# One FP32 inference step on one core: the input projection by seven half-size products in place of eight, and two cache copies issued at another place

## The reference

```
h = rmsnorm(x, norm_mix)                  # (576, 1024): 512 prompt rows, 64 sample rows
z = h @ w_in                              # w_in: (1024, 3072)
q1, q2, k1, k2, va, qb, kb, vb = split(z) # rope on q1, q2, k1, k2, qb, kb
# differential attention on q1..va, dilated window attention on qb, kb, vb
x = x + even_merge(oa, ob) @ w_out        # output projection, (1024, 1024)
x = x + hier_moe(rmsnorm(x))              # top-1 of 4 groups, top-2 of 8 experts; then layer 1
```

## Time and profile before

| | |
|---|---|
| three runs | median 1953.74 us (1950.34 to 1958.75) |
| the profiled execution | 1954.98 us, its span 1953.0 us |
| TensorE products, busy | 1652.9 us (85%) |
| VectorE, ScalarE, GpSimd, busy | 647.7, 329.2, 215.5 us |
| DMA | 659.20 MB, mean 338 GB/s |
| granted TensorE clock, mean | 0.928 |

### The profile page before, as it was taken

The page is one execution under the profiler, slowest core; times in us unless marked ns, Lnnn a source line. Parts: engine busy times, 40 slices in busy tenths (PEclk is TensorE's granted clock), DMA queues, the critical chain, the costliest instruction groups (busy, mean ns, idle before and its releaser), DMA issues.

```text
span 1953.0 us, 32634 instructions
## 1 busy us (share of the span) xinstructions
PE 1652.9 (85%) x12820; PEld 784.3 (40%) x12820; DVE 647.7 (33%) x1326; ACT 329.2 (17%) x753; POOL 215.5 (11%) x356
## 2 busy tenths in 40 slices
PE   8999898888898887887788879998968887877785
PEld 4444355555445322222223347764532222323231
DVE  3213468777514300000000159984160000000005
ACT  2000245444302000000000020004120000000001
POOL 1001122232200100000000021000020000000000
PEclk9999989899898899999989889999979999999997
DMA  9999489999853899999999999704169999999995
GB/s 341 346 362 349 176 307 336 348 355 366 345 220 135 321 428 428 410 429 427 427 427 428 415 267 324 248 13 170 65 251 426 428 419 422 427 428 428 427 422 210
DMA packets 83830, 659.20 MB, mean 338 GB/s; under 512 B 15308, under 2 KB 15437, under 8 KB 45419
## 3 DMA queue, kind: packets, MB, share of 16 engines
q1 hardware_dynamic: 58906, 569.86, 73.5%
q0 software_dynamic: 24800, 87.65, 11.8%
HBM read 643.18 MB, written 96.53 MB: 379 GB/s over the span
## 4 chain that ended last, share of the span: by engine, by line
PE 55%; DMA 32%; DVE 7%; issue 3%; ACT 2%; SPq 1%; DVEq 0%; ACTq 0%; POOLq 0%
DMA ring<-in 31%; PE ps L2113 15%; PE ps L1758 10%; PE ps L2068 7%; PE ps L2276 6%; PE ps L1716 4%; PE ps L1882 2%; PE ps L2297 2%; PE ps L2133 2%; PE ps L1867 1%; DVE ring L1238 1%; PE ps L1822 1%; DVE ring L1231 1%; PE ps L1798 1%; DMA ring<-y_rows 1%
## 5 line engine op out<-in xcount | busy, mean ns | idle before, releaser
L2113 PE MATMUL ps<-ring,big 128*32 128x512 f32 (+1 forms) x2688 | 477.6, 654 | 129.2 <-DMA ring<-in 123.3
L2113 PEld LDWEIGHTS ps<-ring,big 128*32 128x32 f32 (+1 forms) x2688 | 148.4, 132 | 453.8 <-issue 386.4
L1433 DVE TENSOR_TENSOR big<-big,ps 128x512 f32<-128x512 f32 x32 | 22.0, 689 | 821.9 <-PE ps L2113 778.6
L2133 PE MATMUL ps<-ring,big 128*32 128x512 f32 (+1 forms) x928 | 215.7, 606 | 21.3 <-DMA ring<-in 12.8
L767 ACT ACTIVATE big<-ps 128x512 f32<-128x512 f32 (+4 forms) x136 | 74.2, 547 | 737.0 <-PE ps L1716 403.2
L1758 PE MATMUL ps<-ring,act_t 128*128 128x512 f32 (+1 forms) x480 | 191.5, 597 | 4.0 <-DMA ring<-in 3.6
L2068 PE MATMUL ps<-ring,big 128*128 128x512 f32 (+1 forms) x288 | 124.2, 614 | 5.7 <-ACT big L1127 4.8
L2276 PE MATMUL ps<-act_t,ring 128*128 128x288 f32 x512 | 124.4, 406 | 0.0
L1758 PEld LDWEIGHTS ps<-ring,act_t 128*128 128x128 f32 (+1 forms) x480 | 78.4, 181 | 100.5 <-issue 96.0
L2133 PE MATMUL ps<-act_t,big 128*32 128x512 f32 (+1 forms) x416 | 99.0, 594 | 14.0 <-ACT big L767 12.4
L2276 PEld LDWEIGHTS ps<-act_t,ring 128*128 128x128 f32 x512 | 97.3, 190 | 26.8
(11 more groups left out here) (299 smaller groups left out, 1615.4 us busy)
## 6 DMA issues: line engine op xcount, KB each, us to landing
ring<-in SPq DMA_DIRECT2D x180, 2048.0 KB, 18.5
out<-in SPq DMA_DIRECT2D x16, 4080.0 KB
ring<-in SPq DMA_DIRECT2D x128, 256.0 KB, 7.5
ring<-in POOLq DMA_DIRECT2D x128, 256.0 KB, 6.6
act_t<-in SPq DMA_DIRECT2D x16, 2048.0 KB
ring<-in SPq DMA_DIRECT2D x28, 1024.0 KB, 10.9
ring<-in SPq DMA_DIRECT2D x24, 512.0 KB, 6.3
ring<-in POOLq DMA_DIRECT2D x24, 512.0 KB, 4.9
```

Source lines behind the costliest of these rows:

```text
L2113: ins = mm(ps[half, i, :], XgT[:, par_, k, half], slot(eslots(w)[i], 8)[:, k, :], start=(k == 0), stop=(k == KC - 1))
L2133: ins = mm(ps[half, 5 + h, :], hbT[:, k, half], down_weights(w, odd)[:, k, h * 512:(h + 1) * 512], start=(k == 0), stop=(k == 3))
```

## The change

The chunks are paired (0,1), (2,3), (5,4). For each pair ("wave") the 512 prompt rows by 1,024 inputs and the 1,024 inputs by two chunks of 512 columns are seen as 2 x 2 blocks A and B, and the four output blocks are made by seven block products (Strassen's scheme in the form with seven products and common sums), each for two row tiles, with 4 chunks of 128 inputs instead of 8. The sample rows keep the full product. VectorE makes the sums of blocks of A once (`sum1`, `sum2`, `sum4`, and one in place in `act_t`), four sums of blocks of B per wave (`col1` and three in place in the ring slots, each 128 x 2,048), and adds the products up (14 additions of 128 x 512 a wave), the rope behind each. ScalarE copies the first product and the sample rows, and takes over the copies of turned tiles (`z_turned`) from VectorE. Lambda and router preparation moves into wave 2 (index 1). Copies 8 and 9 of the caches leave the place behind the page keys and go ahead of the wait for the load of slot 2 in the output projection. GpSimd's first value pages wait for product `p7_1` of the last wave. The bank for the third row transpose changes (`NORM_BANK`).

```diff
+    col1 = [B(8192, 2048, 4, 512), B(8192, 2048, 4, 512), RG(5120, 2048, 4, 512)]
+    half_sum = [B(11264, 1024, 2, 512), B(11264, 1024, 2, 512), RG(7168, 1024, 2, 512)]
+    sum4 = [B(10240, 1024, 4, 256), B(10240, 1024, 4, 256), act_t[:, 4:8, 0:256]]
...
-    Z_UNITS = [u for q in (0, 2, 4) for u in [((q, t),) for t in range(4)] + [((q, 4), (q + 1, 4))] + [((q + 1, t),) for t in range(4)]]
+    Z_PAIR = (("c11_0", 0, 0), ("sample0", 0, 4), ("sample1", 1, 4), ("c11_1", 0, 1), ("c12_0", 1, 0), ("c12_1", 1, 1),
+              ("c22_0", 1, 2), ("c22_1", 1, 3), ("c21_0", 0, 2), ("c21_1", 0, 3))
+    Z_CHUNKS = ((0, 1), (2, 3), (5, 4))
...
@@ SyncE
-        sp.wait_ge(z_mm, 1)
+        sp.wait_ge(z_mm, Z_MM[0, "p1_1"])
         for i in range(4):
             copy_window(i)
-        sp.wait_ge(z_mm, 9)
+        sp.wait_ge(z_mm, Z_MM[0, "p4_1"])
...
-        sp.wait_ge(z_mm, 18)
+        sp.wait_ge(z_mm, Z_MM[1, "p4_1"])
         pages_in(sp, pages, 0, ck, Kd, kd_in)
-        for i in range(8, 10):
-            copy_window(i)
...
                     elif s < 4:
+                        if s == 2:
+                            for i in range(8, 10):
+                                copy_window(i)
                         sp.wait_ge(p_mm, (5, len(P_UNITS))[s - 2])
@@ VectorE
+        def z_sum(w, name, product, n, t, bank, half=None):
+            k = Z_ROPED.index((n, t)) if (n, t) in Z_ROPED else None
+            if k is not None and half is not None:
+                if k > 3:
+                    dve.wait_ge(z_tr, k - 3)
+                if stores_before(k) > 0:
+                    dve.wait_ge(z_out[k % 4], 16 * stores_before(k))
+            dve.wait_ge(z_mm, Z_MM[w, product])
+            place = z_merged(n, z_place(n, t, k))
+            V.tensor_tensor(place, z_split(n, ps[:, bank, :]), place if half is None else z_split(n, half),
+                            ALU.add).then_inc(dve_ready, 1)
+            if k is not None and name[:2] != "u4":
+                dve.wait_ge(dve_ready, Z_DVE[w, name])
+                roped(n, t)
...
+            V.tensor_tensor(col1[w], b12, b11, ALU.subtract).then_inc(dve_ready, 1)
+            dve.wait_ge(z_copy, Z_ACT[w, "p1_0"])
+            z_sum(w, "c11_0", "p2_0", one_, 0, 6, half_sum[w][:, 0, :])
+            dve.wait_ge(z_mm, Z_MM[w, "sample"])
+            dve.wait_ge(dve_ready, Z_DVE[w, "t1"])
+            V.tensor_tensor(b11, b22, col1[w], ALU.subtract).then_inc(dve_ready, 1)
+            for j in range(2):
+                dve.wait_ge(z_copy, Z_ACT[w, f"sample{j}"])
+                roped(Z_CHUNKS[w][j], 4)
...
+            z_sum(w, "c11_1", "p2_1", one_, 1, 4, half_sum[w][:, 1, :])
...
+            with_half("u2_0", 0, 5, "p6_0")
+            z_sum(w, "u4_0", "p5_0", two_, 0, 6, half_sum[w][:, 0, :])
+            V.tensor_tensor(b12, b22, b12, ALU.subtract).then_inc(dve_ready, 1)
...
+            z_sum(w, "c12_0", "p3_0", two_, 0, 7)
...
+            V.tensor_tensor(b21, b21, b11, ALU.subtract).then_inc(dve_ready, 1)
+            if w == 1:
+                lambda_and_router()
+                S(V.memset(ps[:, 2:4, :], 0.0))
...
+            for i in range(2):
+                z_sum(w, f"c21_{i}", f"p4_{i}", one_, 2 + i, (4, 6)[i], half_sum[w][:, i, :])
+            if w == 1:
                 turn_window(0, 0)
                 turn_window(0, 1)
-        z_turned(*prev)
         for k in range(4):
             turn_pages(0, k)
         fence()
@@ TensorE
+        def z_product(bank, lhs, rhs):
+            for k in range(4):
+                ins = mm(ps[:, bank, :], lhs[:, k, :], rhs[:, k, :], start=(k == 0), stop=(k == 3))
+            ins.then_inc(z_mm, 1)
...
+                z_product(4 + i, a11[i], b11)
+                if w == 0:
+                    row_turn(0, 1 + i)
+                else:
+                    z_turn(Z_CHUNKS[w - 1][0], 2 + i)
+            if w:
+                summed("c21_1", w - 1)
+            z_product(6, a12[0], b21)
+            if w == 0:
+                row_turn(0, 3)
+                row_turn(0, 4)
+                pe.wait_ge(norm_ev, NT)
...
+            z_product(4, a12[1], b21)
+            z_turn(one_, 0)
+            pe.wait_ge(z_copy, Z_ACT[w, "p1_1"])
+            summed("t2")
+            z_product(5, s2[0], b11)
...
+            z_product(6, s1[0], col1[w])
...
+            z_product(7, s4[0], b22)
+            summed("c11_1")
+            z_product(4, s2[1], b11)
+            summed("u2_0")
+            z_product(5, s1[1], col1[w])
+            z_turn(two_, 0)
+            summed("c12_0")
+            z_product(7, s4[1], b22)
+            summed("u2_1")
+            summed("t3")
+            z_product(4, s3[0], b12)
+            summed("c12_1")
+            z_product(7, s3[1], b12)
+            z_turn(two_, 1)
+            summed("t4")
+            summed("u3_0")
+            z_product(4, a22[0], b21)
+            z_turn(two_, 2)
+            summed("c22_0")
+            z_product(6, a22[1], b21)
+            z_turn(two_, 3)
@@ GpSimd
-            if (n, t) == (5, 0):
-                pool.wait_ge(z_mm, 23)
+            if (n, t) == Z_TILES[-1]:
+                pool.wait_ge(z_mm, Z_MM[2, "p7_1"])
                 pages_in(pool, pages[0:8], 0, cv, Vd, vd_in)
```

More of the change, by code:

```diff
@@ L814, in _ @@
         act.drain().then_inc(norm_sq, 1)
-        act.wait_ge(lam_ready, 3)
+        act.wait_ge(dve_ready, 3)
         scaled_row(3)
         scaled_row(4)
[L818 to L841, removed]
@@ new lines, in _ @@
+        for w in range(3):
+            one_, two_ = Z_CHUNKS[w]
+            for i in range(2):
+                act.wait_ge(z_mm, Z_MM[w, f"p1_{i}"])
+                if w:
+                    act.wait_ge(dve_ready, Z_DVE[w - 1, f"c21_{i}"])
+                copy(half_sum[w][:, i, :], ps[:, 4 + i, :]).then_inc(z_copy, 1)
+                if w:
+                    z_turned(Z_CHUNKS[w - 1][0], 2 + i)
+            act.wait_ge(z_mm, Z_MM[w, "sample"])
+            for j in range(2):
+                z_out_copy(Z_CHUNKS[w][j], 4, ps[TS * j:TS * j + TS, 7, :])
+            if w == 0:
+                act.wait_ge(f_mm, 1)
+                A_(st[:, 20:22], ps[:, 3, 0:2], ACT.Exp).then_inc(lam_exp, 1)
+            z_turned(one_, 0)
+            z_turned(one_, 4)
+            z_turned(two_, 4)
+            z_turned(one_, 1)
+            for t in range(4):
+                z_turned(two_, t)
@@ L1183, in _ @@
         rstd(st[:, 8:10], st[:, 3:5], D)
-        dve.drain().then_inc(lam_ready, 1)
-        turned(0, 1)
-        turned(0, 2)
+        dve.drain().then_inc(dve_ready, 1)
+        for t in range(1, NT):
+            turned(0, t)
         dve.wait_ge(consts_in, 48)
@@ new lines, in lambda_and_router @@
+        def lambda_and_router():
+            dve.wait_ge(lam_exp, 1)
+            link(V.tensor_tensor(st[:, 25:26], st[:, 20:21], st[:, 21:22], ALU.subtract))
+            link(V.tensor_scalar(st[:, 25:26], st[:, 25:26], LAM_INIT, None, ALU.add))
+            link(V.scalar_tensor_tensor(st[:, 24:25], C("coef_lam"), st[:, 25:26], C("coef_one"), ALU.mult, ALU.add))
+            link(V.tensor_scalar(st[:, 25:26], st[:, 25:26], -1.0, None, ALU.mult))
+            link(V.tensor_scalar(st[:, 66:67], PR("subln"), 1.0 - LAM_INIT, None, ALU.mult))
+            for l in range(2):
+                S(V.tensor_tensor(router[:, l], router[:, l], gain[:, 1 + 2 * l, :].unsqueeze(2).broadcast_to((P, KC, 36)),
+                                  ALU.mult))
+            S.done()
@@ L1754, in _ @@
             for k in range(KC):
-                if (i, k) in ((0, 4), (0, 6)):
-                    row_turn(0, k // 2 - 1)
-                for j, (n, t) in enumerate(unit):
-                    ins = mm(ps[unit_rows(t, j), 4 + i % 4, :], act_t[:, k, t * P:t * P + rows(t)], slot(n, 8)[:, k, :],
+                for j in range(2):
+                    ins = mm(ps[TS * j:TS * j + TS, 7, :], act_t[:, k, TP:T], slot(Z_CHUNKS[w][j], 8)[:, k, :],
                              start=(k == 0), stop=(k == KC - 1))
```

188 lines of the change are left out of this document (136 added, 52 removed).

## The result

The changed kernel takes 1969.94 us (median of 8 runs, 1963.88 to 1973.08); the kernel before, run beside it, 1953.46 (8 runs). The ratio is 1.0089 [1.0069, 1.0108]: slower by 0.9%; the medians lie 16.5 us apart. The forecast was 1963.6 with a range of 1946 to 1972. The profiled execution took 1967.08 us, its span 1965.0 against 1953.0.

A forecast was written before the change was run, and what follows sets the result against it. The prediction took TensorE to bound the input projection. Against the profiled 1954.98 us, -4.7 (that stage), +0.7 (clock), +11.3 (stall for x) and +2.6 (slow restart) gave +9.9; forecast 1963.6 us, range 1946 to 1972.

The forecast's parts named there:

- the sum: Likeliest case (0.58): input projection gains 4.7 us, clock loses 0.7, late x costs 11.3 plus 2.6; 1957 to 1969 us.
- the stores of wave 1 hold VectorE: Rival (0.16): at the turn to wave 2, late-landing key stores cost TensorE 10 us instead of 2; 1971.6 us.
- Products: Input projection: half-size products of 8 records take 3.44 us against 6.88 for 16, removing 20.6 us.
- Start of the first wave: Input projection: TensorE idles 2.2, 1.6 and 1.9 us waiting for VectorE's scaling and operand sums; 4.9 us stay.
- Stores of wave 1: Turn to wave 2: VectorE's sum waits for a key store to leave its buffer; TensorE loses 2 us (0 to 4.7).
- End of the stage: Input projection: last product at 202.7, then VectorE's last sum and page transposes; fence at 212.7 instead of 217.41, 4.7 us gained.
- Land in time with no copies about: GpSimd's value pages, started nearly 20 us before the fence instead of 27, still land in time; no cost.
- the whole saving stays: Rival (0.08): page transposes hide in the attention's own waits and x is not late; 1940.7 us.
- The two copies: mechanism: Output projection: DMA engines take whole packets in turn, so the copies' 65 KB packets delay x's 4 KB ones.
- The two copies: size: Output projection: x lands at 582.6, its last 1.1 MB taking 2.6 us; TensorE stalls 11.3 us before the fifth unit.
- Slow restart: Output projection: after the stall for x, TensorE's clock is low; 2.6 us lost.
- A shift of its start is carried on, one for one.: Attention starts from the input projection's fence and passes any shift of its start on in full.

The follow-up runs named there:

- copies_back: The changed kernel with copies 8 and 9 issued behind the page keys again, as in the kernel before; 1952.37 us, ratio 1.0005.
- copies_behind_slot2: The changed kernel with copies 8 and 9 issued behind the load of slot 2 in the output projection, when x has landed; 1951.7 us, ratio 0.9995.
- two and six: The tail cut kernel with the eight early cache copies issued as two and six instead of four and four; 1940.28 us, ratio 0.9942.
- one_copy_moved: The changed kernel with copy 8 back behind the page keys and only copy 9 at the new place; 1955.5 us, ratio 1.0018.
- before_copies_moved: The kernel before with only the move of copies 8 and 9 to the output projection; 1967.38 us, ratio 1.0079.
- the tail cut: Changed kernel, page transposes spread over the last wave, all 16 value pages requested behind the fence; 1944.32 us with copies behind slot 2's load, 1944.56 in their old place.
- smaller_pieces: The changed kernel with copies 8 and 9 each issued as two interleaved halves in pieces of 4,352 bytes; 1952.01 us, ratio 0.9986.
- small_packets: The changed kernel with copies 8 and 9 given as 1,020 adjoining rows of 4 KB instead of 16 of 255 KB; 1970.35 us, ratio 1.0106.

## Why the prediction was right or wrong

**The result lies in its range, 0.3% above the number; the sum was +9.9 us against the profiled execution, and +12.1 came (+16.5 between the medians of the runs).** What happened in the two stages is the likeliest case, *the sum*; but 1969.94 lies 0.9 us above that case's own bounds, 1957 to 1969, and nearer to the 1971.6 of the rival *the stores of wave 1 hold VectorE*. The time alone would not have told the two apart; the timeline does, with 1.94 us lost at that turn and not 10. The two stages come to +10.9 (-4.8 and +15.7) where the sum had +9.2 (-4.7, 11.3 and 2.6), and that the pair's total is close as well is in part luck: +3.7 in the attention, where 0.7 was named, and -2.6 behind the output projection nearly cancel. Point by point:

- *Products.* Right: half-size products follow each other at 3.44 us (198.95 less 195.08, less the transposes' 0.43), so 8 records cost half of 16, and the waves take 20.6 us less.
- *Start of the first wave.* Named idles 2.2, 1.6, 1.9; measured 2.73, 1.26, 1.47, sum 5.5 for 5.7.
- *Stores of wave 1.* Named 2 (0 to 4.7); 1.94 here, 2.94 and 3.69 in `copies_back` and `copies_behind_slot2`, none with two and six. So it scatters by nearly 2 us between executions, and the 2 was a good choice within bounds that hold.
- *End of the stage.* Last product 202.4 for 202.7, fence 212.64 for 212.7. But the first product came 0.7 earlier than the sum assumed (14.45 for 15.18), so the stage is some 0.4 us longer than its working.
- *"Land in time with no copies about", value pages at nothing.* This step failed, without changing the sum. It had the requests nearly 20 us ahead of the fence, where the first goes out at 200.36, 12.3 us ahead, since GpSimd issues the store of 199.70 first. And it asked when the pages land, and not what their issue does to GpSimd's own end. The prediction found VectorE's transposes last and stopped there; the end of GpSimd's drain was 1.6 us behind as second. That is why moving the page transposes alone gave 0.9 us and not 8. The rival "the whole saving stays" needed both out of the way.
- *The two copies: mechanism.* Right: one copy gives 12 us of delay, two give 24, the move alone reproduces it, and pieces of 4 KB take it away. The packet counts agree with the turns: in 553 to 578 of the changed kernel (the view of the queues) there are 165 packets from SyncE's queue, 32 of them under 512 B, and 167 of x's:

```profile
q1 hardware_dynamic: 165, 8.39, 92.3%
q0 software_dynamic: 167, 0.68, 8.0%
```

- *The two copies: size.* This is the term that was mis-sized: "the other 1.1 MB takes 2.6 us, at the 420 GB/s of the full queues". The last packets of the copies lie ahead of 576.5, near the 580.0 named; no packet of any queue lies in 576.5 to 577.5, which is not explained. At 577.5 x had 0.93 MB left where 1.1 was named. But these took 6.7 us (to 584.2), at a DMA share of 0.83 in 579 to 581 and 0.20 in 581 to 584: in this trace the last packets of x did not fill the engines. The trace of before has the same tail: behind the weights (553.5 to 561) x moved its last 1.65 MB in 7.4 us, with 0.47 of the DMA engines busy in 557 to 561. x's queue in 577.5 to 585 of the changed kernel, then in 553.5 to 561 of the kernel before:

```profile
q0 software_dynamic: 260, 0.93, 38.5%
```

```profile
q0 software_dynamic: 435, 1.65, 59.3%
```

  Taken from there, 1.1 MB take 4.9 us, and the stall comes out at 13.6 instead of 11.3. Against the sum, counted from the start of the stage: the end of x came 2.8 us later (44.2 for 41.4: the tail took 4.1 more, what lies ahead of it 1.4 less), the first addition 0.2 later, and the fifth unit was wanted at 29.6 instead of 30.8, since the first 32 products took 15.67 us for 16.91. These are the 4.2 us between 11.3 and 15.5, to 0.1.
- *Slow restart.* Named 2.6; the fifth unit takes 8.57 for 7.09, 1.5 us. In `one_copy_moved`, behind an idle time of only 5.3, it takes 9.80, so the loss does not grow with the idle time. The granted clock says where the difference lies: it is at 0.50 at the start of the unit in both, and is back at 1.00 from 588.5 on, 3.3 us after the start, in the changed kernel, but only from 576 on, 5.8 us after it, in `one_copy_moved`. Why it comes back later there is open. The first 32 products of the stage show the same scatter: they took 16.91 us in before, 15.67 here and 13.97 in `copies_back`. The other term for the clock, 0.7 us behind the fence, can't be told from the scatter of the attention, next below.
- *"A shift of its start is carried on, one for one."* In the profiled pair only 1.1 of the 4.8 us arrive at the output projection. The attention takes 323.8 us in before, 327.4 after, 325.7 in `copies_back`, 326.4 in `copies_behind_slot2` and 329.6 in `before_copies_moved`, whose input projection and attention are those of before. So single executions differ by 6 us there, and one pair can't say whether some of the gain is lost in it. The runs say no more: `copies_back`, with a fence 3.0 us earlier than before, has the ratio 1.0005.
- *Strassen's part.* Expected at 4.0 us net; `copies_back` allows at most 0.12% (2.3 us) of gain by its interval. With the tail cut and the copies in their old place the gain is 8.6 us of the 20.6 (0.9956), and the fence opens 9.7 us earlier than in before (207.68 for 217.41). The tail's two edits were not run on the kernel before, whose fence waits for ScalarE behind the last products, with the transposes long done.

## What to carry to other kernels

A DMA window that stands idle a few microseconds later is not free for a transfer that is issued now: look at what is still in flight, and compare packet sizes, not bytes. Here two copies in packets of 65 KB made a load in packets of 4 KB land 24.4 us later, nearly the whole time of the copies, and the same bytes in small packets 3.2 us. When work is taken from the engine that bounds a stage, list all the others in the order in which they end, drains of the fence included, and not only the next one. Price the end of a load by the end of the same load in the trace: the last 0.93 MB took 6.7 us here, where the rate of full queues gave 2.6 for 1.1 MB.

## What the runs showed of the hardware

- Two queues of the DMA engines took turns by packet although the packets differed 16-fold in size (165 of up to 65,280 bytes, 32 of them tiny, beside 167 of about 4 KB, in 25 us): x got 0.68 MB of 9.07. With pieces of 4,352 bytes it was 245 beside 249, and 1.02 MB of 2.09. This is the rule that the prediction weighed (the Trainium skill, DMA: Bandwidth & Descriptors, Queues, rings and completion order: each engine goes round the queue rows, a whole packet at a time), and the counts of the changed kernel and of `smaller_pieces` agree with it.
- An access pattern of 4 KB rows that lie one behind another was moved in the same large packets as before (120 with 7.74 MB in `small_packets`). The rows that do not touch, in `smaller_pieces`, made small ones.
- The drain of GpSimd ahead of a fence took 2.93 us behind its stores and 5.9 to 6.8 us behind eight more requests of 256 KB, though its own instructions had ended. In the kernel before, where those requests were issued some 20 us ahead of it, it took 3.99.
- SyncE took 23.3 us to issue four copies of 480 pieces each, 1.69 for two of 16 rows, and 1.65 for the two of 1,020 rows that lie one behind another.
